# RWKV tiles of a hybrid decoder trunk: modulation weights in a third ring slot, and the inversion's transposed side of odd heads in the other partition half

## What is computed

```
cond = silu(c)
for l in range(2):
    mod = cond @ w_ada[l] + b_ada[l]          # 1024 x 6144 weights a layer
    sh_m, sc_m, g_m, sh_f, sc_f, g_f = split(mod, 6)
    h = rms_norm(x, gain[l, 0]) * (1 + sc_m) + sh_m
    ...mixers, output projection, experts...

# RWKV-7, per head, token by token (layer 0)
S = S * w_t - (S kk_t) (a_t * kk_t)^T + v_t kt_t^T
y_t = S r_t
```

## Time and profile before

| | us |
|---|---|
| median of 3 runs | 1526.92 (1524.36 to 1527.91) |
| the profiled execution | 1525.61 |
| its span | 1523.9 |

### The profile page before, as it was taken

How to read it: one execution, slowest core, us unless ns; L and a number is a source line. 1 busy time by engine, 2 the same in 40 slices (tenths; PEclk the granted TensorE clock), 3 DMA queues, 4 the chain that set the end, 5 groups by cost and what they waited for, 6 DMA issues and landing times.

```text
span 1523.9 us, 23370 instructions
## 1 busy us (share of the span) xinstructions
PE 1340.7 (88%) x10293; PEld 664.5 (44%) x10293; DVE 625.0 (41%) x953; ACT 302.6 (20%) x496; POOL 76.1 (5%) x231
## 2 busy tenths in 40 slices
PE   6999999588887797899999759998998789999992
PEld 3344444266766445333333344554453453333331
DVE  1134541446664217323323245465723553323324
ACT  3211211333331003000000042432212400000002
POOL 7100000000000000000000020000000000000002
PEclk9999998799999898999999979999999889999996
DMA  9773310442455009899999661111100689999994
GB/s 352 257 269 111 111 55 0 179 132 74 133 168 168 1 0 371 334 423 390 384 426 414 266 249 55 56 56 56 56 1 0 277 347 389 418 353 426 424 373 179
DMA packets 87793, 332.70 MB, mean 218 GB/s; under 512 B 6504, under 2 KB 37516, under 8 KB 70284
## 3 DMA queue, kind: packets, MB, share of 16 engines
q1 hardware_dynamic: 74336, 290.04, 49.0%
q10 hardware_dynamic: 7884, 21.24, 3.5%
q0 software_dynamic: 5472, 19.93, 3.5%
HBM read 308.65 MB, written 22.54 MB: 217 GB/s over the span
## 4 chain that ended last, share of the span: by engine, by line
PE 66%; DVE 15%; DMA 12%; ACT 4%; issue 2%; POOL 0%; SPq 0%; DVEq 0%; ACTq 0%; POOLq 0%
PE banks L1858 15%; PE banks L1382 15%; PE banks L1879 9%; DVE work L1994 6%; PE banks L1774 6%; PE banks L1371 3%; DMA h_features<-in_w_ada_dram 3%; DMA h_features<-in_w_up_dram 3%; DMA h_features<-in_w_down_dram 2%; PE banks L1304 2%; PE banks L1758 2%; DMA work<-h_rows,idx_tok 2%; DVE work L2000 1%; DMA ring<-in_w_ada_dram 1%; PE banks L1837 1%
## 5 line engine op out<-in xcount | busy, mean ns | idle before, releaser
L1382 PE MATMUL banks<-h_features,ring 128*128 128x512 f32 x640 | 287.2, 605 | 5.6 <-ACT h_features L976 4.1
L1858 PE MATMUL banks<-ring,work 128*64 128x512 f32 (+1 forms) x672 | 203.3, 602 | 3.9 <-issue 2.3
L1858 PE MATMUL banks<-work 128*64 128x512 f32 (+1 forms) x672 | 199.6, 595 | 0.0
L1382 PEld LDWEIGHTS banks<-h_features,ring 128*128 128x128 f32 x640 | 121.3, 193 | 153.7 <-issue 147.5
L1994 DVE TENSOR_TENSOR work<-work,banks 128x256 f32<-128x256 f32 (+2 forms) x82 | 44.8, 569 | 173.3 <-PE banks L1858 132.6
L1858 PEld LDWEIGHTS banks<-ring,work 128*64 128x64 f32 (+1 forms) x672 | 60.6, 129 | 104.2 <-issue 99.5
L1879 PE MATMUL banks<-ring,work 128*64 128x512 f32 (+1 forms) x288 | 98.7, 593 | 3.5 <-DMA h_features<-in_w_down_dram 2.9
L1774 PE MATMUL banks<-y_features,ring 128*128 128x512 f32 x192 | 85.4, 607 | 6.4 <-DVE small L2515 6.4
L1994 DVE TENSOR_TENSOR work<-work 128x512 f32<-128x512 f32 (+8 forms) x168 | 86.1, 513 | 11.8 <-ACT work L1169 3.6
L1858 PEld LDWEIGHTS banks<-work 128*64 128x64 f32 (+1 forms) x672 | 59.7, 130 | 68.9 <-issue 65.4
L861 POOL DMA_INDIRECT work<-h_rows,idx_tok x20 | 19.0, 951 | 1221.4 <-DVE idx_tok L2651 899.0
(11 more groups left out here) (366 smaller groups left out, 1727.8 us busy)
## 6 DMA issues: line engine op xcount, KB each, us to landing
ring<-in_w_up_dram SPq DMA_DIRECT2D x16, 2048.0 KB, 14.4
work<-in_w_gate_dram SPq DMA_DIRECT2D x16, 2048.0 KB, 13.5
work<-in_w_up_dram SPq DMA_DIRECT2D x14, 2048.0 KB, 14.3
h_features<-in_w_ada_dram SPq DMA_DIRECT2D x24, 1024.0 KB, 5.9
ring<-in_w_down_dram SPq DMA_DIRECT2D x12, 2048.0 KB, 14.2
work<-in_w_down_dram SPq DMA_DIRECT2D x8, 2048.0 KB, 14.2
h_features<-in_w_down_dram SPq DMA_DIRECT2D x8, 2048.0 KB, 14.1
ring<-in_w_ada_dram SPq DMA_DIRECT2D x7, 2048.0 KB, 12.5
```

Source lines behind the costliest of these rows:

```text
L1382: ins = mm(PS[0:w, b, :], lhsT=W[:, k, c0:c0 + w], rhs=h[:, k, :], start=(k == 0), stop=(k == KD - 1))
L1858: ins = mm(PS[rows, bank, :], lhsT=xt[:, k, rows], rhs=w[:, k, :], start=(k == 0), stop=(k == KD - 1))
```

## The change

*Modulation weights.* The load plan gets four entries `("tile", 0, t)` that all fall in ring slot 2. Such an entry holds 512 columns, the weights of units 2 and 3 of tile t. It is loaded when unit 3 of the tile before is summed. Units 0, 1, 4 and 5 stay in `h_features`: 0 and 1 are loaded when units 4 and 5 of the tile before are summed, 4 and 5 when units 0 and 1 of the same tile are. `w_out` piece 0 now follows tile 3's unit 3 in slot 2.

*Inversion.* Output of products and of the transposed side goes to partition half c XOR q (`crossed`): for odd heads it is the other half than the chunk's. T's own side stays in half c. The transposed side of `TTm` for odd heads thus lives crossed, and level 0 computes it with eight matmuls of its own (`first_crossed`). Products are one group of 16 for both q, with one ACT copy of 2x256 columns. The sides are split by side and no longer by q: `upper_side` (T), then `lower_side` (transposed, left out in level 4, where nothing reads it), each with one VectorE merge. The pair of PSUM banks that takes the products alternates with the level (`level_banks`).

```diff
+    for t in range(T // P):
+        plan += [("tile", 0, t), None, None]
+    plan += [("out", 0, i) for i in range(2)]
...
+        def crossed(ap, q, j, c, w=0):
+            return unit(ap, q, j, c ^ q, w)
+        def level_banks(n):
+            p = 2 - 2 * (n % 2)
+            return PS[:, p:p + 2, :], PS[:, 2 - p:4 - p, :]
...
+                elif i > GATE_HALVES:
+                    sp.wait_ge(sem("unit_summed"), unit_done(*(tile_half(t, m - 4) if m >= 4 else tile_half(t - 1, m + 4))))
...
+                    elif kind == "tile":
+                        sp.wait_ge(sem("unit_summed"), unit_done(*tile_half(i, 3)))
...
-                    if PLAN[n] == ("out", 0, 1):
-                        for i in range(GATE_HALVES, HALVES):
-                            load_half(i)
                     if PLAN[n] is not None:
                         load(n)
+                        kind, _, t = PLAN[n]
+                        if kind == "tile":
+                            for m in (0, 1, 4, 5):
+                                load_half(tile_half(t, m)[1])
...
-                    for q in range(2):
-                        act.wait_ge(sem("g_ready"), 10 * t + 2 * n + q + 1)
-                        act.activation(Gq[:, q, :], PS[:, 2 + q, 0:256], ACT.Copy).then_inc(sem("g_copied"), 1)
+                    act.wait_ge(sem("g_ready"), 5 * t + n + 1)
+                    act.activation(Gq, level_banks(n)[0][:, :, 0:256], ACT.Copy).then_inc(sem("g_copied"), 1)
...
+                def products(n):
+                    pe.wait_ge(sem("inv_ready"), 12 * t + (2 * n + 2 if n else 2))
+                    for j, q, c in every():
+                        ins = mm(crossed(level_banks(n)[0], q, j, c), lhsT=unit(Xq, q, j, c), rhs=unit(TTm, q, j, c),
+                                 start=True, stop=True)
+                    ins.then_inc(sem("g_ready"), 1)
+                def first_crossed():
+                    for j in range(4):
+                        for c in range(2):
+                            cs = slice(64 * c, 64 * c + 64)
+                            ins = mm(crossed(PS[:, 0:2, :], 1, j, c, 1), lhsT=SG[t % 2][64:128, j, cs],
+                                     rhs=BE[t % 2][64:128, j, cs], start=True, stop=True)
+                    ins.then_inc(sem("p_ready"), 1)
+                def upper_side(n):
+                    pe.wait_ge(sem("inv_ready"), 12 * t + 2 * n + 3)
+                    pe.wait_ge(sem("g_copied"), 5 * t + n + 1)
+                    for j, q, c in every():
+                        ins = mm(unit(level_banks(n)[1], q, j, c), lhsT=crossed(TTm, q, j, c, 1),
+                                 rhs=crossed(Gq, q, j, c), start=True, stop=True)
+                    ins.then_inc(sem("p_ready"), 1)
+                def lower_side(n):
+                    for j, q, c in every():
+                        ins = mm(crossed(level_banks(n)[0], q, j, c, 1), lhsT=crossed(Gq, q, j, c),
+                                 rhs=crossed(TTm, q, j, c, 1), start=True, stop=True)
+                    ins.then_inc(sem("p_ready"), 1)
...
                 for n in range(5):
-                    for q in range(2):
-                        products(n, q)
+                    products(n)
+                    if n == 0:
+                        first_crossed()
                     if n < 2:
                         score(t, n + 1)
                     else:
                         next_unit(t, 2 * (n - 2))
-                    for q in range(2):
-                        both_sides(n, q)
+                    upper_side(n)
+                    if n < 4:
+                        lower_side(n)
...
+                dve.wait_ge(sem("p_ready"), 10 * t + 1)
+                signal(dve.copy_predicated(four(TTm[:, 1, :])[:, 1], bc(pair64[1][:, 1, :], 4, 1).bitcast(I32),
+                                           four(PS[:, 1, :])[:, 1]), "inv_ready")
...
-                    for q in range(2):
-                        dve.wait_ge(sem("p_ready"), 10 * t + 2 * n + q + 1)
-                        signal(dve.copy_predicated(four(TTm[:, q, :]), bc(pair64[LV[n + 1]], 4, 2).bitcast(I32),
-                                                   four(PS[:, q, :])), "inv_ready")
+                    for w in range(2 if n < 4 else 1):
+                        dve.wait_ge(sem("p_ready"), 10 * t + 2 * n + w + 2)
+                        signal(merged(n, w, level_banks(n)[1 - w]), "inv_ready")
```

More of the change, by code:

```diff
@@ L105, in chunk_plan @@
     plan += [("in", 0, i) for i in range(4, 7)]
-    plan += [None, None, None] + [("out", 0, i) for i in range(2)]
+    for t in range(T // P):
+        plan += [("tile", 0, t), None, None]
+    plan += [("out", 0, i) for i in range(2)]
     plan += [("in", 1, i) for i in range(6)] + [("out", 1, i) for i in range(2)]
@@ L603, in tile_half, with tile_part @@
             return ("half", GATE_HALVES + TILE_HALVES * t + i)
+        def tile_part(i):
+            return divmod(i - GATE_HALVES, TILE_HALVES) if i >= GATE_HALVES else (0, i)
         FIRST_UNITS = 1
@@ L610, in unit_weights @@
             if what == "half":
+                t, m = tile_part(i)
+                if i >= GATE_HALVES and m in (2, 3):
+                    return ring_ap(("tile", 0, t))[:, :, 256 * (m - 2):256 * (m - 1)]
                 return half_place(i)
@@ L1291, in ada_sums @@
                 what, i = unit
-                if what == "half":
+                t, m = tile_part(i)
+                if what == "half" and i >= GATE_HALVES:
+                    if m in (2, 3):
+                        arrived(pe, ("tile", 0, t))
+                    else:
+                        before = (3, 2)[m % 2] + 2 * t + m // 4
+                        pe.wait_ge(sem(f"half_loaded{m % 2}"), 16 * (before + 1))
+                elif what == "half":
                     pe.wait_ge(sem(f"half_loaded{i % 2}"), 16 * (i // 2 + (2 if i % 2 == 0 else 1)))
@@ L1543, in next_unit, with every @@
                     ada_sums(tile_half(t, i))
-                def products(n, q):
-                    pe.wait_ge(sem("inv_ready"), 12 * t + 2 * n + q + 1)
+                def every():
+                    return [(j, q, c) for j in range(4) for q in range(2) for c in range(2)]
+                def products(n):
[4 more added lines that the diff above has]
+                    ins.then_inc(sem("g_ready"), 1)
@@ L2292, in score_copy @@
                            "score_copied")
-                    for q in range(2):
-                        signal(dve.copy_predicated(four(TTm[:, q, :]), bc(pair64[1], 4, 2).bitcast(I32),
-                                                   four(PS[:, 5 + q, :])), "inv_ready")
+                    signal(dve.copy_predicated(four(TTm[:, 0, :]), bc(pair64[1], 4, 2).bitcast(I32),
+                                               four(PS[:, 5, :])), "inv_ready")
+                    signal(dve.copy_predicated(four(TTm[:, 1, :])[:, 0], bc(pair64[1][:, 0, :], 4, 1).bitcast(I32),
+                                               four(PS[:, 6, :])[:, 0]), "inv_ready")
                 elif n == 1:
@@ L2307, in inversion, with merged @@
             def inversion(t):
+                dve.wait_ge(sem("p_ready"), 10 * t + 1)
+                signal(dve.copy_predicated(four(TTm[:, 1, :])[:, 1], bc(pair64[1][:, 1, :], 4, 1).bitcast(I32),
+                                           four(PS[:, 1, :])[:, 1]), "inv_ready")
+                def merged(n, w, banks):
+                    half = slice(256 * w, 256 * w + 256)
+                    return dve.copy_predicated(eight(TTm[:, :, half]),
+                                               bc(bc(pair64[LV[n + 1]][:, w, :], 4, 1), 2, 1).bitcast(I32),
+                                               eight(banks[:, :, half]))
                 for n in range(5):
```

17 lines of the change are left out of this document (4 added, 13 removed).

## The result

The changed kernel takes 1516.75 us (median of 16 runs, 1510.96 to 1522.40), the one before 1524.02 us beside it. The ratio is 0.9949, with a 95% interval of 0.9935 to 0.9963. By the ratio that is 7.8 us less (the two medians differ by 7.3), where 26 were forecast. The direction was right; the time lies outside the range given (1492 to 1512).

The account below looks back on a forecast made before the run. It took TensorE's waits for modulation weights in the RWKV inversions as the bound, with VectorE next. Tiles 0 to 3 gave -8.8 -5.9 -5.9 -8.0, clock dips +2.6: -26.0 us, so 1501 us, range 1492 to 1512.

Parts of the forecast that it names:

- What bounds the kernel: RWKV inversions: TensorE waits twice per tile for weights, 3.2% of the span (48.8 us); VectorE bounds levels 0 and 1.
- Four corners: Inversion matmuls: products and both sides run four corners at once, products 0.94 to 0.53 us, sides 1.90 to twice 0.53.
- The inversions' layout: Inversions of tiles 0 to 3, timed engine by engine: 22.0, 24.5, 24.5 and 23.8 us.
- ACT's front piece 0: Tiles with a next tile's front: this 4.4 us piece delays the G copy of level 3, a new wait.
- The step that failed: From VectorE's first Un of the solve to the next tile's start, 13 us were carried over unchanged.
- its twin for w_out: Last tile: w_out issued at about 479, both pieces in some 10 us before the output projection needs them.
- The clock: Tiles 1 and 2: idle in levels 0 and 1 brings one clock dip each, +1.3 us each, +2.6 in all.
- rival C: RWKV stage: less-busy TensorE idles more, another two clock dips a tile at 1.6 us; 1514 us, chance 10%.
- Rival D: Inversions: loads in flight together make units 4 and 5 wait 3 us a tile; 1513 us, chance 8%.
- Rival B: Inversion matmuls: only two corners at once when row halves share a PSUM bank; 1509 us, chance 15%.
- E: RWKV stage: clock stays at 1.2 GHz through most of it, slower than before; 1615 us, chance 3%.
- Range: Whole kernel: 1492 to 1512 us, meant to hold for 8 in 10.

Follow-up runs that it names:

- e1: Only the weights part of the change, with the inversion of the kernel before; ratio to before 1.0008.
- e2: Only the inversion part of the change, with the weight loads of the kernel before; ratio to before 1.0038.
- e7: Small loads: changed kernel, transferring only 16 columns of one row group for most modulation weights; only the RWKV stage is readable, 183.9 us against 204.0.
- e4: Changed kernel with the loads of tiles 1 to 3 (2 MB, units 0 and 1) issued in levels 0 and 1; ratio to before 0.9948.
- e12: Changed kernel with only w_out's two pieces loaded later; ratio to before 0.9943, tail 23.0 us instead of 28.0.
- e9: Changed kernel with the small loads of e7 plus unread matmuls in TensorE's waits; only the RWKV stage is readable, 184.4 us.

## Why the prediction was wrong, point by point

- **What bounds the kernel.** Right: the waits for weights were on the chain and are gone but for one piece in tile 3; VectorE bounds levels 0 and 1. That the three matters (loads, matmuls, clock) hang together was missed: e1 and e2 show that neither part gains alone.
- **Four corners.** Right for products and upper side: 0.5 to 0.6 us from a group's start to the next one's in tile 1, 0.53 laid out. Wrong for the lower side: "the change spreads all three groups over four corners" overlooks that it reads and writes the same half. Its 0.53 us measured 0.9.
- **The inversions' layout.** Mis-sized by 7.0 us of 94.8 in the changed kernel; with small loads by 2.7, of which the lower sides are an estimated 2. The other 4.3 are in tiles 1 to 3, which start with a dip in the changed kernel and without one in e7. ACT's front piece 0, the one new wait that I named, was on the chain.
- **The step that failed** is "from there to the next tile's start nothing is touched, and that stretch (13 us) I carry over whole", with its twin for w_out, costed at nothing because its bytes arrive in time. The rests grew by 19.9 us over the forecast. What the change puts there are transfers: the 2 MB and two 1 MB loads now run for the first 10 us of tile 0's solve (before, two 1 MB loads for 6 us), and w_out's 4 MB during the last one. I asked of each transfer when it lands and what waits for it, and not what runs meanwhile. What ran meanwhile stalled for 7.9 us and fell to half clock. e7 shows the stretch at 18.4 us when the transfers are away, e4 when they are moved elsewhere, e12 shows 5 us for w_out in the tail.
- **The clock.** The term was +2.6 us by the wrong trigger. Its idle stretches in levels 0 and 1 cause no dip in tiles 1 and 2 of e7. 31 us more at half clock came, most of it behind stalls, 10 us at the starts of tiles 1 to 3; rival C (1514 us, 10%) was the nearest to the outcome, and its reason, a TensorE with less to do, is only half of it: e1, with the full matmul time of before, has 20.5 us too.
- **Rival D** (loads still late) is out: 0.6 us of such waits in the stage. **Rival B** is out by the records. **E** is out as well.
- **Range.** It took in B but stopped short of C and D, at 1513 and 1514; the result was 1516.75. Instruction supply was in no rival, although the trace of before had a stall of that kind of 0.36 us in a matmul group.

What stays open: which part of the 20 us that e7 gives back is stall, which the clock behind it, and whether a stall sets off the dip in every case. Five dips follow a stall; three (358.6, 406.4, 457.6) come where TensorE waited for VectorE, and the same wait brings none in e7. Two stalls (388.8, 483.7) have no dip behind them.

## What to carry to other kernels

A transfer that is hidden from its reader can still lengthen code that has nothing to do with it: when loads move into a stretch of short matmuls, look for "issue" idle in it and don't carry that stretch over at its old length. When matmuls are spread over the corners of the array, work out row half and output half for every group from its operands. Two parts of a change that relieve the same loop from two sides may each be worth nothing or less alone (1.0008 and 1.0038 here) and pay together; test both halves before judging one. Once a wait is removed, TensorE's clock can take part of the gain: filling its waits with unread matmuls is a cheap test, and here, with w_out moved, it brought the gain from 0.5% to 1.2%.

## What the runs showed of the hardware

Every stall ends 2.2 to 2.8 us after a packet of the instruction queue starts; this holds for all 23 of 0.3 us or more in the changed kernel, e4, e7 and e9, with transfers or without. In the changed kernel one starts in 483.00 to 483.25 us and the stall at 483.67 ends at 485.47; one in 489.25 to 489.50, end 491.67. In e4_late one at 369.0 to 369.25, and the 3.6 us stall ends at 371.42. The DMA view of 483.0 to 483.5 (queue: packets, MB, share of 16 engines):

```profile
q1 hardware_dynamic: 92, 0.19, 98.6%
q8 instruction: 1, 0.02, 12.4%
```

The packet carries 16 KB and takes 12.4% of 16 engines for 0.5 us, 1.0 us, no longer than one in a quiet stretch (33.4% of 0.25 us at 492.75, 1.3 us). So it isn't slower under load; if it is what TensorE waits for, it begins too late. In the changed kernel all seven stalls have the weights' queue at 62 to 106% of the engines in the quarter of a us in which their packet starts; of the 18 packets that start in the stage with that queue at 0%, none is followed by one. But in e7 and in e9 two such quiet packets are followed by a stall. Nor are transfers enough: in the kernel before, eight packets start with the 16 engines over 80% busy in the half us ahead, and none is followed by a stall. That the late block is what TensorE waits for is inferred from these times; no run changed the instruction queue by itself. The Trainium skill (Runtime: NRT & Kernel Launch, Instruction fetch mechanics) says that instructions are refilled in blocks of 16 KiB by the sequencer's own DMA queue, and that crossing a block is mostly hidden. The instruction queue in the profile, 80 packets and 1.31 MB, agrees with the size; in this stage, with 7.9 of 204 us, crossing isn't hidden, if the late block is the cause.
